# Down products of the first block in PSUM banks 4 to 7, and the last norm tile by tile with two stores

## What is computed

```python
def swiglu(x, w_gu, w_d):
    a, b = jnp.split(x @ w_gu, 2, axis=-1)
    return (jax.nn.silu(a) * b) @ w_d

def first_block(...):                       # DFF = 2816 = 22 * 128, DEPTH = 2
    h = x
    for l in range(DEPTH):
        f = swiglu(rmsnorm(h, g[0]), w_ffn_gu[l, 0], w_ffn_down[l, 0])
        h = h + 0.5 * rmsnorm(f, g[1])
        ...                                 # mixing: mLSTM, spatial gating, attention, w_out
        f = swiglu(rmsnorm(h, g[4]), w_ffn_gu[l, 1], w_ffn_down[l, 1])
        h = h + 0.5 * rmsnorm(f, g[5])
    return h

def second_block(...):
    for li in range(DEPTH):
        ...                                 # mixer, then an MLP with squared ReLU, gated, added to xl
    return rmsnorm_2(xl, norm_f_g)          # the last norm: x * rsqrt(mean(x*x) + eps) * g
```

## Time and profile before

| | |
|---|---|
| median of 3 runs | 3442.36 us (3441.5 to 3445.35) |
| profiled execution | 3442.04 us, its span 3440.3 us |
| PE busy | 3123.4 us (91% of the span) |
| DVE busy | 2106.2 us (61%) |
| ACT busy | 1395.0 us (41%) |
| mean granted TensorE clock | 0.948 |

### The profile page before, as it was taken

The page is one execution under the profiler, slowest core; times in us unless marked ns, Lnnn a source line. Parts: engine busy times, 40 slices in busy tenths (PEclk is TensorE's granted clock), DMA queues, the critical chain, the costliest instruction groups (busy, mean ns, idle before and its releaser), DMA issues.

```text
span 3440.3 us, 53748 instructions
## 1 busy us (share of the span) xinstructions
PE 3123.4 (91%) x22184; PEld 2703.9 (79%) x22184; DVE 2106.2 (61%) x3021; ACT 1395.0 (41%) x2009; POOL 285.2 (8%) x330
## 2 busy tenths in 40 slices
PE   8999999998999999899896788878999899896897
PEld 8987887897987788798683677766888678785785
DVE  6876646686886654688436677744333466675554
ACT  5455444445445544444423333323222344313443
POOL 2000000000000000000101022211000001051000
PEclk9999999999999999999998799979999999987999
DMA  9865645786966555596420000012332133400453
GB/s 266 281 186 157 174 148 173 229 265 213 274 206 185 143 172 159 180 280 223 142 61 1 1 9 3 3 56 64 97 98 93 61 96 93 118 1 31 142 177 133
DMA packets 450059, 463.91 MB, mean 135 GB/s; under 512 B 18096, under 2 KB 346992, under 8 KB 449840
## 3 DMA queue, kind: packets, MB, share of 16 engines
q1 hardware_dynamic: 428336, 385.07, 37.6%
q0 software_dynamic: 21504, 75.72, 6.6%
HBM read 459.68 MB, written 1.05 MB: 134 GB/s over the span
## 4 chain that ended last, share of the span: by engine, by line
PE 76%; DVE 15%; ACT 5%; issue 3%; DMA 1%; POOL 0%; DVEq 0%; SPq 0%; ACTq 0%; POOLq 0%
PE banks L317 21%; PE banks L319 20%; PE banks L318 20%; DVE weights_lo L303 1%; PE banks L4401 1%; PE banks L3622 1%; DVE arena L4047 1%; ACT weights_hi L295 1%; PE banks L3646 1%; PE banks L1308 1%; DVE arena L1454 1%; PE banks L4443 1%; DVE first_input_split L1319 1%; PE banks L3762 1%; DVE third_weights_split L303 1%
## 5 line engine op out<-in xcount | busy, mean ns | idle before, releaser
L303 DVE TENSOR_TENSOR weights_lo<-raw_weights,weights_hi 128x1024 fp32r<-128x1024 f32 (+3 forms) x399 | 471.3, 1183 | 336.4 <-ACT weights_hi L295 308.4
L295 ACT ACTIVATE weights_hi<-raw_weights 128x1024 fp32r<-128x1024 f32 (+3 forms) x399 | 408.4, 1026 | 556.3 <-PE banks L319 536.1
L268 DVE TENSOR_TENSOR weights_lo<-raw_weights,weights_hi 128x1024 fp32r<-128x1024 f32 x180 | 223.1, 1241 | 475.2 <-ACT weights_hi L261 285.8
L261 ACT ACTIVATE weights_hi<-raw_weights 128x1024 fp32r<-128x1024 f32 x180 | 190.6, 1060 | 519.5 <-PE banks L319 513.4
L317 PE MATMUL banks<-first_input_split,weights_hi 128*128 128x256 f32 (+1 forms) x1204 | 344.0, 286 | 10.5 <-DVE first_input_split L1319 4.3
L319 PE MATMUL banks<-first_input_split,weights_lo 128*128 128x256 f32 (+1 forms) x1204 | 341.9, 284 | 0.0
L318 PE MATMUL banks<-first_input_split,weights_hi 128*128 128x256 f32 (+1 forms) x1204 | 339.8, 282 | 0.0
L317 PE MATMUL banks<-work_split,weights_hi 128*128 128x512 f32 (+2 forms) x776 | 271.7, 350 | 17.9 <-DVEq L2492 14.1
L303 DVE TENSOR_TENSOR third_weights_split<-raw_weights,third_weights_split 128x1024 fp32r<-128x1024 f32 (+1 forms) x173 | 208.1, 1203 | 120.7 <-ACT third_weights_split L295 105.3
L319 PE MATMUL banks<-work_split,weights_lo 128*128 128x512 f32 (+2 forms) x776 | 269.9, 348 | 0.0
L295 ACT ACTIVATE third_weights_split<-raw_weights 128x1024 fp32r<-128x1024 f32 (+1 forms) x173 | 179.8, 1039 | 222.1 <-PE banks L319 220.2
(11 more groups left out here) (609 smaller groups left out, 7254.0 us busy)
## 6 DMA issues: line engine op xcount, KB each, us to landing
raw_weights<-in_w_ffn_gu SPq DMA_DIRECT2D x176, 512.0 KB, 5.4
raw_weights<-in_w_in SPq DMA_DIRECT2D x144, 512.0 KB, 3.6
raw_weights<-in_mlp_w SPq DMA_DIRECT2D x128, 512.0 KB, 3.9
arena<-in_ada_w POOLq DMA_DIRECT2D x96, 512.0 KB, 5.5
raw_weights<-in_w_ffn_down SPq DMA_DIRECT2D x80, 512.0 KB, 3.6
raw_weights<-in_w_branch SPq DMA_DIRECT2D x48, 512.0 KB, 3.4
raw_weights<-in_ssd_w_in SPq DMA_DIRECT2D x48, 512.0 KB, 3.9
raw_weights<-in_w_mkv SPq DMA_DIRECT2D x32, 512.0 KB, 4.0
```

What stands on the lines that cost most here:

```text
L261: last = s.activation(self.w_hi[:, u % 2, :], self.raw[:, u, :], ACT.Copy)
L268: last = v.tensor_tensor(self.w_lo[:, u % 2, :], self.raw[:, u, :], self.w_hi[:, u % 2, :].bitcast(F32), ALU.subtract)
L295: last = s.activation(hi, raw, ACT.Copy)
L303: last = v.tensor_tensor(lo, raw, hi.bitcast(F32), ALU.subtract)
```

## The change

In the first block the down products of all four feed-forwards gather in banks 4 to 7 (`4 + 2 * part + half`). The rows stretch gets `late=2`: TensorE waits at its start only until all but the last two gated stretches are taken. It also gets `ready=side_made`: TensorE waits there for the end of the side chain, which uses banks 4 to 7. ACT gets two new waits in each down projection (`hidden_made`), ahead of unit 0 for all but the last two gated stretches and ahead of unit 16 for all of them. `add_normed` reads from bank 4 after a feed-forward and from bank 0 after the mixing output; the transposes of `normed_input` go to the banks just read, and the mixing's first keys move from bank 6 to bank 2.

At the end, the gain of the last norm is fetched by POOL behind the last MLP's gate and ahead of its `modulated_input`. The last norm runs tile by tile, each on its own chain: Square and sum, Sqrt with eps as its bias, reciprocal, product. The store is two DMAs of 512 KB, each behind its own tile, on one semaphore.

```diff
@@ class Stream @@
         while self.split < min(n, len(self.todo)):
             stretch, u = self.todo[self.split]
+            if u in (0, stretch.last_of) and stretch.pieces[0] is not None:
+                self.hidden_made(0 if u else 2)
             self.c.split_unit(*stretch.units[u], stretch.pieces[u])
             self.split += 1
+
+    def hidden_made(self, late):
+        c = self.c
+        made = c.taken - late
+
+        @c.block.scalar
+        def _(s):
+            s.wait_ge(c.taken_by_vector, made)
@@ def rows_stretch(c, hidden, k_chunks, w_rows, ready) @@
-            last = c.three_products(pe, c.ps[:, 2 * part + half, :], staged[:, 0, tokens],
+            last = c.three_products(pe, c.ps[:, 4 + 2 * part + half, :], staged[:, 0, tokens],
...
-    stretch = Stretch(units, product, whole=True, pieces=[hidden[:, k:k + 1, :] for k in ks])
+    stretch = Stretch(units, product, whole=True, late=2, ready=ready, pieces=[hidden[:, k:k + 1, :] for k in ks])
+    stretch.last_of = ks.index(16)
@@ def product_rows @@
-def product_rows(c, t):
-    return c.ps[:, 2 * t:2 * t + 2, :]
+def product_rows(c, t, bank):
+    return c.ps[:, bank + 2 * t:bank + 2 * t + 2, :]
@@ def normed_input(c, gain, x, stream, arrived=None, first=4) @@
-        feature_major(c, ch, c.y[:, t, :], x, t, 2 * t, front=True)
+        feature_major(c, ch, c.y[:, t, :], x, t, first + 2 * t, front=True)
@@ def first_block @@
-        return Stream(c, up + [rows_stretch(c, hidden, 22, w_down)])
+        return Stream(c, up + [rows_stretch(c, hidden, 22, w_down, side_made)])
+
+    def side_made():
+        end = chain_end(c.side)
+
+        @c.block.tensor
+        def _(pe):
+            pe.wait_ge(*end)
...
-        out = [Stretch(feature_units(w_mkv, [0, P]), from_memory[0], first_keys, ready=memory_ready, fixed=6)]
+        out = [Stretch(feature_units(w_mkv, [0, P]), from_memory[0], first_keys, ready=memory_ready, fixed=2)]
...
-        add_normed(c, done, slots[1], 0.5)
+        add_normed(c, done, slots[1], 0.5, 4)
...
-        add_normed(c, done, slots[0], 1.0)
+        add_normed(c, done, slots[0], 1.0, 0)
...
-        normed_input(c, slots[1], x_in, stream)
+        normed_input(c, slots[1], x_in, stream, first=0)
...
-        add_normed(c, done, slots[2], 0.5)
+        add_normed(c, done, slots[2], 0.5, 4)
+def final_norm(c, gain, result):
+
+    ss = cols(c.small, 0, NT)
+    chains = c.rows_chains[:NT]
+    c.loaded()
+    try_root(c)
+    for t, ch in enumerate(chains):
+
+        @ch.block.scalar
+        def _(s):
+            s.wait_ge(ch.steps_done, ch.steps)
+            s.activation(result[:, t, :], c.h[:, t, :], ACT.Square, scale=1.0 / 32,
+                         accum_out=ss[:, t:t + 1]).then_inc(ch.steps_done, 1)
+        ch.steps += 1
+        root_of_mean(c, ch, ss[:, t:t + 1])
+        reciprocal_of(c, ch, ss[:, t:t + 1])
+
+        @ch.block.vector
+        def _(v):
+            v.wait_ge(ch.steps_done, ch.steps)
+            v.scalar_tensor_tensor(result[:, t, :], c.h[:, t, :], ss[:, t:t + 1], gain, ALU.mult,
+                                   ALU.mult).then_inc(ch.steps_done, 1)
+        ch.steps += 1
+    return result, chain_ends(chains)
@@ def second_block @@
         gate = Gate(c, layer, 5, tiles // NT, cols(c.par, 2 * D, 2, D))
+        if last_layer:
+            final_gain = c.par[:, 0:D]
+            c.load(final_gain, a["norm_f_g_2"].partition_broadcast(P))
         modulated_input(c, layer, 1, tiles, y4, *wide(c, tokens))
...
-    joined(c, c.rows_chains)
-    final_gain = c.par[:, 0:D]
-    c.load(final_gain, a["norm_f_g_2"].partition_broadcast(P))
-    c.loaded()
-    result = cols(c.work, 0, NT, D)
-    c.rmsnorm(tiles_of(c.h), tiles_of(result), final_gain)
-    c.result = result
+    c.result, c.result_ends = final_norm(c, final_gain, cols(c.work, 0, NT, D))
@@ def program @@
-            sp.wait_ge(c.steps_done, last)
-            sp.dma_start(out.rearrange("o (t p) d -> p (o t) d", p=P), c.result).then_inc(c.result_stored, 16)
-            sp.wait_ge(c.result_stored, 16)
+            for t, (semaphore, value) in enumerate(c.result_ends):
+                sp.wait_ge(semaphore, value)
+                sp.dma_start(rows[:, t, :], c.result[:, t, :]).then_inc(c.result_stored, 16)
+            sp.wait_ge(c.result_stored, 16 * NT)
```

More of the change, by code:

```diff
@@ L964, in __init__ @@
         self.emitted, self.numbers, self.banks = False, {}, None
+        self.last_of = None
 class Stream:
@@ L1158, in bank_features, with rows_stretch @@
     return c.ps[:, banks:banks + 2, :].rearrange("p b (j t) -> p (b j) t", t=SEQ)
-def rows_stretch(c, hidden, k_chunks, w_rows):
+def rows_stretch(c, hidden, k_chunks, w_rows, ready):
     w_v = w_rows.rearrange("(k p) n -> p k n", p=P)
@@ L1214, in reciprocal_of, with add_normed @@
     ch.steps += 1
-def add_normed(c, done, gain, scale):
+def add_normed(c, done, gain, scale, bank):
     def gained(t, semaphore, value):
@@ L1224, in _ @@
             v.wait_ge(semaphore, value)
-            v.scalar_tensor_tensor(two_halves(c.y[:, t, :]), product_rows(c, t), scale, two_halves(gain.buf),
+            v.scalar_tensor_tensor(two_halves(c.y[:, t, :]), product_rows(c, t, bank), scale, two_halves(gain.buf),
                                    ALU.mult, ALU.mult).then_inc(c.rows_gained, 1)
@@ L1235, in _ @@
             s.wait_ge(ch.steps_done, ch.steps)
-            s.activation(two_halves(c.junk[:, t, :]), product_rows(c, t), ACT.Square, scale=1.0 / 32,
+            s.activation(two_halves(c.junk[:, t, :]), product_rows(c, t, bank), ACT.Square, scale=1.0 / 32,
                          accum_out=c.ss[:, t, 0:1]).then_inc(ch.steps_done, 1)
@@ L1258, in add_normed, with normed_input @@
         ch.steps += 1
-def normed_input(c, gain, x, stream, arrived=None):
+def normed_input(c, gain, x, stream, arrived=None, first=4):
     for t, ch in enumerate(c.tile):
@@ L4689, in program @@
         second_block(c, a)
-        last = c.steps
+        rows = out.rearrange("o (t p) d -> p (o t) d", p=P)
         @block.sync
         def _(sp):
-            sp.wait_ge(c.steps_done, last)
-            sp.dma_start(out.rearrange("o (t p) d -> p (o t) d", p=P), c.result).then_inc(c.result_stored, 16)
-            sp.wait_ge(c.result_stored, 16)
+            for t, (semaphore, value) in enumerate(c.result_ends):
+                sp.wait_ge(semaphore, value)
+                sp.dma_start(rows[:, t, :], c.result[:, t, :]).then_inc(c.result_stored, 16)
+            sp.wait_ge(c.result_stored, 16 * NT)
 def kernel(**inputs):
```

## The result

The changed kernel takes 3427.79 us (median of 12 runs, 3422.53 to 3441.79) against 3441.93 us of the kernel before (12 runs beside it). The ratio is 0.9948, with a 95% interval from 0.9931 to 0.9964. Set on the 3442.36 us shown ahead of the prediction, the ratio gives 3424.5 us, 17.9 us less; the two medians differ by 14.1 us. The forecast was 3428.3 us and 14.0 us less, in a range from 3424.5 to 3434.0. The direction and the sum held; by the ratio the time came out at the very lower edge of the range and, unrounded, just under it (3442.36 x 0.9948 = 3424.46).

A forecast was written before the change was run, and what follows sets the result against it. TensorE's long row of matmuls with gaps was taken as the bound. 6.0 us at the gated-to-down changes plus 8.0 at the end, 14.0 off 3442.04, gave 3428.0, with 0.3 for the median 3428.3 us; range 3424.5 to 3434.0.

The forecast's parts named there:

- Bound and places: Whole kernel: TensorE's matmuls bound it, so gains come only in its gaps on the chain or at the end; 14.0 us.
- part 1: First block's four changes from gated to down units: down products in banks 4 to 7 with late=2 gain 6.0 us.
- parts 2 and 3: Kernel's end: early gain fetch, norm tile by tile and two stores together gain 8.0 us (bounds 6.8 and 8.1).
- What is late next: Gated-to-down changes: unit 0 starts 1.95 us earlier, but unit 1 waits for L305, leaving 1.1 us at the first.
- Change 2 and its clock: Second gated-to-down change: without idle time ahead of unit 0 the clock stays up, gain 2.7 us; 1.95 if it falls.
- Banks, waits of ScalarE, the side wait at no cost: First block: the moved banks, ACT's two new waits and TensorE's wait for the side chain cost nothing.
- The early fetch: Last norm's gain, fetched behind the last MLP's gate: 4.47 us go from the end, 0 lost at the new place.
- The norm by tiles and the stores: Kernel's end: first store issued at 3427.6, second at 3429.12, span ending 3.2 us later at 3432.3 against 3440.33.
- A: Whole kernel: the gains come as summed, 3428.3 us (3426 to 3431 with bounds of store and wake-up); chance 0.60.
- D: More gained than summed: unit 1 doesn't bind or another gap shrinks behind the down units, to 3424.9 us; chance 0.10.
- B: Clock falls in unit 0 at every gated-to-down change, which then gain 3.1 us together: 3431.2 us; chance 0.15.
- E: Slower through TensorE's granted clock, more falls in the second block's gaps, only by chance: 3450 us; chance 0.04.

The follow-up runs named there:

- e6: Changed kernel with down unit 1's splitting written ahead of the taking of the last gated stretch; ratio 0.9948 against the kernel before.
- e2: Kernel before with only the new end (early gain fetch, norm tile by tile, two stores), old first block; 3436.23 us, ratio 0.9969.
- e3: Changed kernel with late=0 in the down stretch, so TensorE's old wait stays with the new banks and end; 3437.02 us, ratio 0.997.
- e5: Kernel before with only the last norm's gain fetched ahead of the last MLP's input; 3456.22 us, ratio 0.9986.
- e4: Changed kernel with one store of 1 MB behind both tiles instead of two of 512 KB; 3427.64 us, ratio 0.9944.
- e7: Changed kernel with unit 1 split earlier, plus last products and stores in column halves (four stores of 256 KB); ratio 0.9959 against the kernel before.
- e1: Changed kernel with the old end, so only the first block's part (banks, late=2, waits); 3437.3 us, ratio 0.9964 against the kernel before.
- e0: Changed kernel run again without edit, beside its own parts on one chip; 3429.9 us, ratio 0.9957 against the kernel before.
- e9: Repetition without edit of the kernel with unit 1 split earlier and four stores of 256 KB; ratio 0.9946 against the kernel before.

## Why the prediction was right in its working and too narrow in its range

**Bound and places: right.** All of the gain that comes back in every trace lies in the four gaps ahead of the down units and behind the last matmul: 13.9 us against a sum of 14.0. That the two agree to 0.1 us is in part luck: part 1 was put 0.3 too high (6.0, measured 5.7), parts 2 and 3 0.2 too low (8.0, measured 8.2).

**What is late next: right.** Unit 0 starts at once, unit 1 then waits for L305 and starts 0.05 us behind its end as said, and the gain is 1.02 to 1.08 us (1.1 said) and not 1.95. e6 shows the cause by taking it away: the rest of the gap and of what it costs, 1.05 us each, comes once unit 1 is split earlier. The later units do not bind, as said: unit 2 of the first change is ready 0.35 us ahead of its start in the trace after, and unit 3 has more.

**Change 2 and its clock: right in this trace, less sure than it was put.** It gained 2.60 us (2.7 said). Four traces have the old wait (before, e2, e3, e5), sixteen idle times of 1.95 us in all. The low clock stands behind four of them: at change 2 in before, e2 and e5 (unit 0 takes 4.44 us each time), and at change 3 in e2 (4.46 us). In the eight traces without the wait, 32 changes, it never stands in the units 0 to 4. So the idle time goes with the fall, but doesn't force it, and the place isn't fixed either. The three traces with the old first block differ at change 3 with the same instructions; the missing fall in e3 could also be due to its banks, which no run separates. A removed fall is worth 1.6 us, and the four traces have one each in the mean (1, 2, 0 and 1), so 5.7 us for part 1 is also their mean, by few traces. The Trainium skill says in "TensorE: Matmul & The Clock Gate", Part 1, that the same kernel can differ between runs; change 3 in e2 against before and e5 agrees with it.

**Banks, waits of ScalarE, the side wait at no cost: right.** e3 has all of them and shows no loss at any change, and no gain at 1, 3 and 4.

**The early fetch: right.** 4.40 us of the 4.47 said, no cost at its new place.

**The norm by tiles and the stores: right, slightly small.** 8.17 us against 8.0; the end came 3.0 us behind the second store's issue (3421.2 to 3424.2) where 3.2 was taken. The Trainium skill asks in "DMA: Bandwidth & Descriptors", rules for kernel authors, for a megabyte or more in each DMA; for the last store of this kernel the runs go the other way: e4 shows that the second store gains 1.44 us, and e7 that four gain 0.46 over two even so. For these stores, issued by SyncE, the part that doesn't shrink is 1.3 to 1.4 us of the landing (2.0, 2.6 and 4.0 us for 256, 512 and 1024 KB, with their data at 400 GB/s; an estimate). The Trainium skill has about 2 us for it in "DMA: Bandwidth & Descriptors", Anatomy of one DMA, fitted to DMAs that GpSimd issues; the prediction took that figure over for SyncE's stores.

**The failed step: the spread from run to run, put at nothing in "The range holds A, D from 3424.5 up and B up to 3434.0".** Each bound of that range is a bound of a term of the sum. The granted clock entered it as rivals of the four changes (B) and as a loss that "only chance would do" with 4 in 100 (E); that the same chance could make the comparison come out 4 us too good has no term. The runs showed a gain of 17.9 us by the ratio, with an interval from 12.4 to 23.8, where the traced places give 13.9 and the medians of the same runs 14.1. Set on the 3442.36 us, the ratio gives 3424.46 us, 0.04 under the lower bound; the medians would give 3428.2, well inside the range. So the mechanism doesn't fail here, and that the time fell just outside rather than just inside is chance. The spread behind it: 27 of 97 runs of the old kernel are 14.5 us longer, by one stretch at the lower clock as far as the traces tell, and within the lower group the runs spread over 12 us. The hint was on the page: three runs shown ahead of the prediction differed by 3.9 us, and the clock row has five of forty slices at 7 or 8, all in the second block. I read them as a property of the program and not as a spread that the measurement would bring in. The half width of the ratio's interval, 5.7 us, set around the sum gives 3422.6 to 3434.1.

The ratios of the parts seem to contradict the sum: e1's and e2's stand for 12.4 and 10.7 us, together 23, against 14.8 for both parts in one (e0), while their traces add up to 5.7 + 8.2 = 13.9. Among the runs without the long stretch, all four kernels on one chip, the excess is a common one: e0, e1 and e2 lie 16.0, 7.6 to 8.7 and 10.4 us under the kernel before, each some 2 to 3 us more than its traced 13.9, 5.7 and 8.2. (The 8.7 leaves out e1's highest run, 3446.3 us, which could be of either group.) e1 and e2 share no edit, so a steady gain in both would show twice in e0, and it shows once. Measured from e0 instead, e2 lies 5.6 us above it, where the first block's part is 5.7, and e1 7.3 to 8.3, where the end's part is 8.2. So what is 2 us off is most likely the median of the kernel before in that sitting; why, no run shows.

## What to carry to other kernels

Where a wait goes, look in program order for what the two engines behind it do next: here the gap closed only by 1.0 to 1.1 of 1.95 us, because the next unit's splitting stood behind the work waited for, and exchanging two lines brought the rest. At the end of a kernel count each step that has no need of the last result, fetch it early, and let the last transfer be small: a store of 512 KB behind the last product instead of 1 MB was worth 1.4 us. And before giving a range for a change of a few thousandths, ask how far the same kernel is from itself: here the traced gaps came back within 0.1 us from trace to trace, where the ratio of 12 runs to 12 had 5.7 us to either side.

## What the runs showed of the hardware that was not expected

TensorE's granted clock can fall for long in a stretch in which the engine is busy for 97% of the time (28.27 of 29.00 us), mostly with matmuls of 64 columns: 0.69 instead of 1.00, and 0.50 over 30 us of it. In e2 the engine was busy for all of the 12 us ahead of that, at 1.00. It costs 13.9 to 14.1 us, in some executions and not in others of the same program (e7 and e9 are one kernel; e9's trace has it, e7's hasn't), always in the same matmuls. The runs of the kernel before come in two groups 14.5 us apart, which it most likely makes. What decides between them was not tried; the kernel's own edits here were all outside that stretch.

A store of 512 KB behind the last product ended the kernel 1.44 us sooner than one of 1 MB, and 256 KB another 0.46 us sooner.
